# Hybrid pool/mLSTM DiT block on one core: when VectorE makes the modulation sums of the second layer, how their weights are fetched, and how the recurrence's rows lie in DRAM

## The reference, cut to what matters

```python
for i in range(2):                       # x: 1024 tokens x 1024, ctx: 256 tokens x 1024
    sh1, sc1, gt1, sh2, sc2, gt2 = split(silu(c) @ mod_w[i] + mod_b[i])      # 6 x 1024, and again for c_ctx
    hx = rms_norm(x) * (1 + sc1) + sh1   # hc likewise from ctx
    yx = pool_mixer(hx) if i == 0 else mlstm_mixer(hx, hc)
    x = x + gt1 * rms_norm(yx)
    x = x + gt2 * rms_norm(conv_ffn(rms_norm(x) * (1 + sc2) + sh2))
    # layer 0 updates ctx in the same way

def mlstm_mixer(hx, hc):
    qk, v, o, gates = split(h @ w_in)    # 8 heads, 64 wide for q and k, 128 for v
    q, k = split(silu(dwconv(qk)))       # 3x3 taps on the token grid
    # chunks of the sequence: state C, n, m carried from chunk to chunk, forward and backward
    d_w = exp(b[t] - b[s] + ig[s] - m_t);  s = (q @ k.T) * d_w
    h = (s @ v + a_t * (q @ C_prev)) / max(|den|, exp(-m_t))
    return (sigmoid(o) * (h_fwd + h_bwd)) @ w_out
```

## Time and profile before

| | us |
|---|---|
| median of 3 runs | 2312.73 (2310.48 to 2315.27) |
| the profiled execution | 2315.27 |
| its span, first to last instruction | 2313.5 |
| PE busy / DVE busy / ACT busy / POOL busy | 2215.1 / 1514.5 / 1009.1 / 1024.0 |
| mean granted TensorE clock | 0.985 of full speed |

### The profile page before, as it was taken

One profiled execution on the slowest core, in us unless ns is written; L12 is line 12 of the kernel. 1 busy time (PEld: TensorE's weight loads), 2 busy tenths in 40 slices (PEclk: granted clock), 3 DMA queues, 4 the chain that ended last, 5 costly groups with the idle time before them and its releaser, 6 DMA issues.

```text
span 2313.5 us, 35556 instructions
## 1 busy us (share of the span) xinstructions
PE 2215.1 (96%) x13230; PEld 1843.3 (80%) x13230; DVE 1514.5 (65%) x1994; ACT 1009.1 (44%) x1633; POOL 1024.0 (44%) x612
## 2 busy tenths in 40 slices
PE   7989999999999999999899998889999999999997
PEld 5657788888888889998699997767778888888885
DVE  5487566667797735454573536743577777888886
ACT  4653344444444465544332323333464444444443
POOL 0036777777600056652211105630397777771002
PEclk9999999999999999999999999989999999999998
DMA  8764432222381476542242168722112222228352
GB/s 340 249 223 169 159 127 100 82 82 82 132 302 41 163 270 229 168 157 85 97 139 73 61 199 212 208 82 74 64 43 94 82 82 82 109 100 288 131 173 101
DMA packets 144147, 326.85 MB, mean 141 GB/s; under 512 B 11408, under 2 KB 65296, under 8 KB 131728
## 3 DMA queue, kind: packets, MB, share of 16 engines
q1 hardware_dynamic: 126448, 299.87, 38.1%
q10 hardware_dynamic: 17568, 25.17, 3.0%
HBM read 269.82 MB, written 55.18 MB: 140 GB/s over the span
## 4 chain that ended last, share of the span: by engine, by line
PE 86%; DVE 4%; ACT 3%; DMA 3%; POOL 2%; issue 2%; SPq 0%; ACTq 0%; DVEq 0%; POOLq 0%
PE ps L1446 11%; PE ps L1448 11%; PE ps L1447 11%; PE ps L1076 6%; PE ps L1575 6%; PE ps L1078 6%; PE ps L1077 6%; PE ps L1577 5%; PE ps L1576 5%; PE ps L1619 2%; PE ps L1621 2%; PE ps L1620 2%; PE ps L1774 1%; PE ps L1214 1%; PE ps L1350 1%
## 5 line engine op out<-in xcount | busy, mean ns | idle before, releaser
L3117 DVE SCALAR_TENSOR_TENSOR acc<-ps,fcv,acc 128x945 f32<-128x945 f32 (+2 forms) x320 | 391.2, 1222 | 82.2 <-ACT acc L2296 49.6
L3857 POOL TENSOR_TENSOR w_lo<-raw,w_hi 128x2048 fp32r<-128x2048 f32 x36 | 170.2, 4728 | 387.1 <-ACT w_hi L2077 272.7
L3916 POOL TENSOR_TENSOR p_s_lo<-p_s_val,p_s_hi 128x512 fp32r<-128x512 f32 x160 | 242.7, 1526 | 116.0 <-ACT p_s_hi L2240 115.7
L1575 PE MATMUL ps<-da_hi,dw_hi 128*128 128x512 f32 x560 | 218.8, 391 | 0.0
L1576 PE MATMUL ps<-da_hi,dw_lo 128*128 128x512 f32 x560 | 218.1, 389 | 0.0
L1577 PE MATMUL ps<-da_lo,dw_hi 128*128 128x512 f32 x560 | 217.9, 389 | 0.0
L1619 PE MATMUL ps<-w_hi,hx_hi 128*128 128x256 f32 x512 | 146.1, 285 | 4.3 <-ACT stage L2649 4.2
L1621 PE MATMUL ps<-w_hi,hx_lo 128*128 128x256 f32 x512 | 145.6, 284 | 0.0
L1620 PE MATMUL ps<-w_lo,hx_hi 128*128 128x256 f32 x512 | 145.5, 284 | 0.0
L1575 PEld LDWEIGHTS ps<-da_hi,dw_hi 128*128 128x128 f32 x560 | 105.1, 188 | 23.2 <-issue 1.6
L1577 PEld LDWEIGHTS ps<-da_lo,dw_hi 128*128 128x128 f32 x560 | 105.1, 188 | 21.9
(11 more groups left out here) (515 smaller groups left out, 6513.8 us busy)
## 6 DMA issues: line engine op xcount, KB each, us to landing
f_raw<-in_ffn_w SPq DMA_DIRECT2D x25, 1024.0 KB, 5.0
modw<-in_modw SPq DMA_DIRECT2D x48, 512.0 KB, 8.0
raw<-in_ffn_w SPq DMA_DIRECT2D x23, 1024.0 KB, 5.0
a_scr<-fprod SPq DMA_DIRECT2D x40, 512.0 KB, 2.6
land_w<-in_ffn_w SPq DMA_DIRECT2D x40, 512.0 KB, 4.1
f_raw_b<-in_ffn_w SPq DMA_DIRECT2D x18, 1024.0 KB, 5.0
land_b<-a_scr SPq DMA_DIRECT2D x30, 512.0 KB, 5.0
raw<-in_mlstm_w SPq DMA_DIRECT2D x14, 1024.0 KB, 5.1
```

The lines of the kernel that those rows point to most:

```text
L1575: pe.matmul(out, dw_hi[r][:, ws], da_hi[r][:], start=begins, stop=False, skip_group_check=True)
L3117: dve.scalar_tensor_tensor(out, src, cv[:, t:t + 1], out, ALU.mult, ALU.add).then_inc(sem("tap_done"), 1)
L3916: pool.tensor_tensor(p_lo[p][:], src, p_hi[p][:].bitcast(F32), ALU.subtract).then_inc(S.sem("lo_in"), 1)
```

## The change

It has four parts.

- DVE makes the modulation halves in other places: 0 to 3 ahead of all taps, 4 to 7 behind m = 1, 8 to 11 behind m = 3, 12 and 13 behind m = 5, 14 to 19 behind the taps and ahead of the gates, 20 to 23 behind the gates. SP's bursts are placed so that one or two halves always lie loaded ahead.
- The recurrence's rows go to DRAM only for x units and only for the heads' rows, in two new arrays, so that what a unit fetches is one run: 4096 bytes for `dmat`, 2048 for `qa`. There are 7 writes in place of 5.
- All four first `rows_in` are issued together, and the wait for the last `stage` stores moves from ahead of the first one to behind the values of units 4 and 5.
- The transfers of the output weights, `mo_raw` (1 MB) and two of 512 KB into `raw`, move from ahead of unit 6 and ahead of the first values to u = 14, 15 and 16.

```diff
-HALVES_BEHIND = {1: (0, 4), 3: (4, 10), 5: (10, 14)}
-HALVES_LOADED = {2: (0, 2), 6: (2, 6), 7: (6, 12), 9: (12, 16), 13: (16, HALVES)}
+HALVES_BEHIND = {-1: (0, 4), 1: (4, 8), 3: (8, 12), 5: (12, 14)}
+HALVES_LOADED = {3: (0, 6), 5: (6, 10), 7: (10, 14), 9: (14, 16), 11: (16, 20), 12: (20, 22), 13: (22, HALVES)}
...
-            for n, name in enumerate(("gcum", "greset")):
-                sp.dma_start(row_scr[n][:, 0:TC], gk[name][0:64, :]).then_inc(sem("rows_out"), 16)
-                sp.dma_start(row_scr[n][:, TC:NT], gx[name][0:64, :]).then_inc(sem("rows_out"), 16)
+            for dr in range(2):
+                rows = slice(32 * dr, 32 * dr + HEADS)
+                sp.dma_start(decay_scr[dr, 2:NCH].rearrange("n h t -> h n t"), gx["gcum"][rows, :].rearrange("h (n t) -> h n t", t=CH))\
+                    .then_inc(sem("rows_out"), 16)
+                for par in range(2):
+                    rows = slice(32 * dr + par, 32 * dr + HEADS, 2)
+                    sp.dma_start(query_scr[dr, 2:NCH, par].rearrange("n h t -> h n t"), gx["greset"][rows, :].rearrange("h (n t) -> h n t", t=CH))\
+                        .then_inc(sem("rows_out"), 16)
...
-            for K in (K_MOUT, K_MOUT + 1):
-                tile_out(K, a["mlstm_w"][K - K_MIN], K % 2)
...
-            for i in range(2):
-                sp.wait_ge(sem(f"stage_out{i}"), run[i])
...
-                src = row_scr[0, 32 * dr:32 * dr + 8, n * CH:n * CH + CH]
-                sp.dma_start(dmat[:, i % 4], src.unsqueeze(0).broadcast_to([P, HEADS, CH])).then_inc(sem(f"row_in{i % 4}"), 16)
+                src = decay_scr[dr, n].rearrange("h t -> (h t)")
+                sp.dma_start(dmat[:, i % 4].rearrange("p h t -> p (h t)"), src.unsqueeze(0).broadcast_to([P, HEADS * CH])).then_inc(sem(f"row_in{i % 4}"), 16)
...
-            rows_in(x_units[0])
-            rows_in(x_units[1])
+            for i in range(4):
+                rows_in(x_units[i])
             sp.wait_ge(sem("unit_done"), 4)
             values_in(4)
             values_in(5)
-            rows_in(x_units[2])
-            rows_in(x_units[3])
+            for i in range(2):
+                sp.wait_ge(sem(f"stage_out{i}"), run[i])
             for u in range(4, len(units)):
-                if u == 6:
-                    sp.wait_ge(sem("unit_done"), 4)
+                if u == 14:
                     sp.wait_ge(sem("modcol1_ready"), M + 2)
                     sp.dma_start(mo_raw[:], a["mlstm_w"][len(MSEQ) + 2][:, 0:2048]).then_inc(sem("mo_in"), 16)
+                if u in (15, 16):
+                    tile_out(K_MOUT + u - 15, a["mlstm_w"][len(MSEQ) + u - 15], (K_MOUT + u - 15) % 2)
...
+            for n in range(*HALVES_BEHIND[-1]):
+                chunk_half(n)
             for m in range(8):
...
+            dve.wait_ge(sem("q_silu"), 8)
+            dve.wait_ge(sem("kc_silu"), 4)
+            for n in range(14, 20):
+                chunk_half(n)
...
-            dve.wait_ge(sem("kc_silu"), 4)
-            for n in range(HALVES_BEHIND[5][1], HALVES):
+            for n in range(20, HALVES):
                 chunk_half(n)
```

More of the change, by code:

```diff
@@ L272, in build @@
         stage = at("stage", WORK + 28672, [P, 2, 256])
-        NT = NCH * CH
+        ROWS_OUT = 16 * 7
         GA = W_HI
@@ L375, in build @@
         o_scr = scratch("o_scr", (8, P, 1024))
-        row_scr = scratch("row_scr", (2, 64, NT))
+        decay_scr = scratch("decay_scr", (2, NCH, HEADS, CH))
+        query_scr = scratch("query_scr", (2, NCH, 2, HEADS // 2, CH))
         al_scr = scratch("al_scr", (64, NCH))
@@ L593, in build @@
              "step_done": 8, "evicted": 8, "res_added": 8, "half_pair0": 192, "half_pair1": 192, "half_pair2": 192, "half_pair3": 192,
[1 row of a table removed]
+             "half_pair4": 64, "landed0": 16, "landed1": 16, "landed2": 64, "b21_in2": ROWS_OUT, "a_out0": 144, "a_out1": 144,
              "first_pair0": 160, "first_pair1": 160, "first_pair2": 160, "first_pair3": 160, "first_pair4": 160})
@@ L937, in _ @@
             sp.wait_ge(sem("rows_ready"), 3)
-            for n, name in enumerate(("gcum", "greset")):
-                sp.dma_start(row_scr[n][:, 0:TC], gk[name][0:64, :]).then_inc(sem("rows_out"), 16)
-                sp.dma_start(row_scr[n][:, TC:NT], gx[name][0:64, :]).then_inc(sem("rows_out"), 16)
+            for dr in range(2):
[6 more added lines that the diff above has]
+                        .then_inc(sem("rows_out"), 16)
             sp.dma_start(al_scr, gend[0:64, 3, :]).then_inc(sem("rows_out"), 16)
-            sp.wait_ge(sem("rows_out"), 80)
+            sp.wait_ge(sem("rows_out"), ROWS_OUT)
             sp.wait_ge(sem("vo_done"), evac_of[len(MSEQ) - 2][-1] + 1)
@@ L973, in rows_in @@
                     sp.wait_ge(sem("num_done"), i - 3)
-                src = row_scr[0, 32 * dr:32 * dr + 8, n * CH:n * CH + CH]
-                sp.dma_start(dmat[:, i % 4], src.unsqueeze(0).broadcast_to([P, HEADS, CH])).then_inc(sem(f"row_in{i % 4}"), 16)
+                src = decay_scr[dr, n].rearrange("h t -> (h t)")
+                sp.dma_start(dmat[:, i % 4].rearrange("p h t -> p (h t)"), src.unsqueeze(0).broadcast_to([P, HEADS * CH])).then_inc(sem(f"row_in{i % 4}"), 16)
                 for par in range(2):
-                    src = row_scr[1, 32 * dr + par:32 * dr + 8:2, n * CH:n * CH + CH]
-                    sp.dma_start(qa[64 * par:64 * par + 64, i % 4],
-                                 src.unsqueeze(0).broadcast_to([64, 4, CH])).then_inc(sem(f"row_in{i % 4}"), 16)
+                    src = query_scr[dr, n, par].rearrange("h t -> (h t)")
+                    sp.dma_start(qa[64 * par:64 * par + 64, i % 4].rearrange("p h t -> p (h t)"),
+                                 src.unsqueeze(0).broadcast_to([64, 4 * CH])).then_inc(sem(f"row_in{i % 4}"), 16)
             def gates_in(u):
@@ L3675, in _ @@
             dve.wait_ge(sem("cols_ready"), 4)
-            dve.wait_ge(sem("rows_out"), 80)
+            dve.wait_ge(sem("rows_out"), ROWS_OUT)
             dve.wait_ge(sem("vo_done"), len(evacs))
```

## The result

| | before | after |
|---|---|---|
| median | 2311.61 us (2310.18 to 2315.27, 4 runs) | 2296.96 us (2295.55 to 2298.81, 4 runs) |
| the profiled execution | 2315.27 us | 2295.55 us |
| its span | 2313.5 us | 2293.7 us |
| mean granted TensorE clock | 0.985 | 0.990 |

The change makes the kernel faster: the ratio is 0.9935, with a 95% interval of 0.9918 to 0.9952. The forecast was 2295.5 us, with a range of 2289 to 2304. In the change PE's lines stand 3 higher: L1097 is now L1100, L1774 is L1777, L1808 is L1811; in the experiments they shift by a few lines either way.

A forecast was written before the change was run, and what follows sets the result against it. PE was taken as the bound, busy 2215.1 of 2313.5 us. Gains of 12.1 + 4.9 + 1.5 = 18.5 us gave 2296.8 from the profiled execution or 2294.2 from the median; 2295.5 was taken between them, range 2289 to 2304.

The forecast's parts named there:

- Term one: Second context norm in the projections: PE no longer waits for DVE's reciprocal, and its clock stays up; 12.1 us gained.
- Cover of the moved sums: Projections: halves 0 to 3 and 14 to 19 fit into DVE's idle time at their new places; 0 us.
- Early traffic: Near 1042 to 1055 us: four more halves (2 MB) move, yet stores get through; 0 us, bounds -7.4 and +2.5.
- Term two: Early recurrence: the third x unit's rows come earlier, so its 11.20 us become 6.32; 4.9 us gained.
- Term three: Recurrence: rows in long runs shorten transfers, ending PE's wait behind the first gates; 1.5 us gained, bounds 0 and 3.
- output weights later: Recurrence from u = 14: 2 MB more in the queue fit, since gated units take longer; 0 us, bound -2.
- The queue's share: Recurrence: the transfer queue's share falls to about three quarters, a unit's transfers from 6.2 to 4.6 us.
- The rival that long runs are served more slowly: Recurrence: 4096-byte runs across 128 partitions slower than short ones; at 8.5 us a unit, time 2333 us; chance 0.03 (slower).
- A sign of being wrong: Recurrence: the prediction would be wrong if POOL still waits for rows in every unit; no size given.
- recurrence gives little: Rival: queue stays as slow with long runs, or late output weights delay gates; gain 12 to 14, about 2301 us; chance 0.15.
- early traffic: Rival: early loads cost the full 7.4 us in the first `o` tile's evacuations; gain 11.1, 2304 us; chance 0.11.

The follow-up runs named there:

- e3: Kernel before with only the loads of halves 2 and 3 issued one weight tile earlier (behind t = 5, not 6): 2300.32 us, ratio 0.9952.
- e1: Kernel before with only the modulation sums and their loads in the new places: 2301.61 us, ratio 0.9961.
- e4: Changed kernel with the output weights fetched in units u = 7, 9 and 11, not 14, 15 and 16: 2296.39 us, ratio 0.9937.
- e7: Changed kernel with only two units' rows ahead of the values of units 4 and 5, the next two behind them: 2299.11 us, ratio 0.9948.
- e10: Changed kernel repeated unedited, in more rounds: 2298.27 us, ratio 0.9938.
- e12: Changed kernel with the two raw transfers moved from u = 15 and 16, so all output weights at u = 14: 2301.78 us, ratio 0.9959.
- e2: Changed kernel with the modulation sums and their loads at the old places: 2307.22 us, ratio 0.9981.
- e8: Changed kernel with sums at old places, old loads except halves 2 and 3 one tile earlier, output weights at u = 7, 9, 11: 2295.95 us, ratio 0.9938.
- e9: Kernel of e11 with the first two gate transfers issued at u = 11 and 12, not 13 and 14: 2295.32 us, ratio 0.9927.
- e11: Kernel of e8 repeated unedited, in more rounds: 2294.60 us, ratio 0.9925.
- e5: Changed kernel with the output weights back at their old places: 2296.96 us, ratio 0.9945.

## Why the prediction was right, and where it was not

- **Term one** (12.1 us, bounds 9.3 to 12.5) was right in mechanism and in size. B to D fell by 58.93 - 49.46 + 244.24 - 241.12 = 12.6 us. From the last product ahead of the spread to the next one it is 11.42 - 1.04 = 10.4 us less, as forecast; the ten products behind took 2.38 us and not 4.12, so the clock gave 1.7 us there, as forecast too. The 0.5 us left lie elsewhere ahead of D and have no cause that I know. e3 shows that the late load alone was the cause.
- **Cover of the moved sums** (0): right. Halves 0 to 3 were done at 1055.8 (forecast 1055), halves 4 to 7 at 1101.4 (forecast 1100.7), halves 14 to 19 at 1275.0, 3.8 us ahead of the gates. The first two loads landed 12.5 and 13.0 us after their issue, though, later than the 10.7 that I took as the worst; the slack took it up. By e3 this move bought nothing, and the forecast didn't see that; it took the table of sums and that of loads as one.
- **Early traffic** (0, bounds -7.4 and +2.5) is a term that I mis-sized. The profiled pair shows 0.3 us, since the kernel before had a moment of low clock there and the changed one none (0.97 against 1.00 on the mean). Over all kernels A to B is 52.0 us on average where four more halves move early (changed, e1, e4 to e7, e10, e12) and 50.3 where they don't (before, e2, e3, e8, e9, e11): a cost of 1.7 us. PE's waits alone say the same, 3.9 against 2.2 us on average. I had argued that the new loads go one at a time, so that stores get through. The four behind the first two do go so, and the stores still landed later, in 2.5 to 4.6 us and not 1.8 to 1.9, which held ACT and with it PE.
- **Term two** (4.9 us, bounds 3.4 to 5.5): right. The unit's interval fell by 11.20 - 6.33 = 4.9 us, 3.4 of it the wait and the rest the clock (0.86 over that interval before), and e7 gives back 3.5. e1 shows how near the edge the old order was: there the same rows at the same place cost only 0.9 us more than an even unit. Why they landed that much better in e1 I can't say.
- **Term three** (1.5 us) was right by itself, and **output weights later** (0, bound -2) is the step that I had wrong, though its bound held. With the weights at their old places, u14 to u16 takes 18.22 us with old rows (e1) and 16.61 with new ones (e5): 1.6 us for the rows, as the first gates reach POOL 1.9 us earlier. With new rows and late weights it is 18.32, 18.66, 18.00 and 16.82 us (changed, e10, e2, e7), 17.95 on average: 1.3 us lost again, and 3.4 with twice the weights (e12). I had argued that gated units are long enough for 2.8 us of `mo_raw`. They are long enough for values and rows; the second gates are issued behind it and landed after 9.5 us. From 1425 to 1450 the queue's share is 90.5% in the changed kernel and 80.2% in e5, which has no weights there. So this part of the change gives back most of what the long runs win, by the traces; the device times of the changed kernel, e4 and e5 don't tell them apart. In e7, with the same order of issue, the second gates landed after 7.9 us, and that is why it escaped; why they were faster there stays open.
- **The queue's share** was forecast to fall to about three quarters, from 6.2 us of transfers for a unit to 4.6. In the stretch without gates or weights it is 66.9 against 77.2%, 13% less. For a unit that is 0.772 x 6.32 = 4.9 us with the old rows and 4.2 with the new. My price of 2.4 ns a packet came from a stretch with gates, whose packets are larger: 623 bytes on average there, 500 here. Per MB both stretches agree, 0.983 x 25 / 6.35 = 3.9 us and 0.772 x 25 / 5.00 = 3.9; the long runs cost 0.669 x 25 / 5.24 = 3.2. The rival that long runs are served more slowly is out. The Trainium skill, page "DMA: Bandwidth & Descriptors", section "Specifications", gives line rate from 512 bytes on. By that the two forms would have cost the same; the measurement differs, by a fifth.
- **A sign of being wrong** that I had named did show: POOL still waits for rows, 1.9 to 3.7 us in each of the sixth to eleventh x unit. It was a poor sign. PE waits for nothing there, before as after, since POOL is ahead of it by then and sits idle until the next buffer of rows has been freed and filled.
- **The sum.** With the measured terms it is 12.6 + 4.9 + 1.6 - 1.7 - 1.3 = 16.1 us, against 14.7 to 14.9 on the medians; the rest, 1.2 to 1.4 us, I can't place. The 18.5 of the forecast was too high by the two costs. The 19.8 us between the two profiled spans are high by chance: the changed kernel's profile has no low clock in the first two x units, where its repetition e10 has one that costs 1.6 us, and the profiled execution of before was 3.7 us above its median. That the time itself was missed by only 1.5 us is partly luck. The gain was forecast 3.9 us too high, but was taken from 2295.5 + 18.5 = 2314.0 us, between the median and the profiled execution, 2.4 us above what the kernel before took.
- **The rivals.** 14.7 us lies just under my 15 to 22 and just over the 12 to 14 of *recurrence gives little*. The recurrence gave its gain, D to E fell by 7.2 us against a forecast of 6.4; but that rival's late weights did push the gates back, as *early traffic* did cost, at a quarter of its full price.

## What to carry to other kernels

When an engine comes late because it sat in a wait for a load, move the load in the issuing queue's list before anything is moved on the engine: one edit of a table gave 11 of the 14.7 us here, and moving the work as well cost about 1.7, by the stages. A bulk load with no due time belongs where the queue has slack and nothing urgent is issued right behind it; in the first turns of a loop, look for the first use of each new stream (here the gates) and keep bulk out of the two turns ahead of it. Cost a transfer's form by the queue's share in a stretch where only that stream moves, and per MB rather than per packet. To tell what ends last in a pipelined unit, line up all kernels: a difference that stays constant, as the 15.0 us here, names the transfer.

## What was unexpected of the hardware

The granted clock falls for a moment around the first x unit in some executions and not in others of the same program. The changed kernel, first x unit, the first profile (its row stands above with 2.05 us) and its repetition e10:

```profile
1385.38 3.65 PE L1777 MATMUL ps<-vch,dmat 128*128 128x129 f32 x16 [0.41 <-DMA vch<-v_scr]
```

In e10 the granted clock from 1380 to 1390 us is 0.83 on the mean, between full speed and the lower level:

```profile
1380.00:1390.00 10.00, 7.42 (x68) 6.51 (x66) 4.08 (x7) 9.49 (x33) 6.16 (x4) 0.83 0.39 107
```

Ahead of it PE does the same in both, with waits of 2.2 us for `dmat` and 0.2 to 0.4 us for the values. The unit then takes 6.32 to 6.33 us (changed, e5, e8), 6.84 to 6.96 (before, e4, e11) or 7.25 to 7.96 (the others), so 1.6 us come and go with no edit. In e5 the moment lies ahead of the unit, in before, e4 and e11 partly so: from D to the second x unit it is 25.0 us in the changed kernel and e8, and 26.2 to 27.9 in all others. A similar one sits between u = 17 and 19 in the profiles of before and of the changed kernel, an interval of 9.95 us where it is 8.3. What decides it stays open.

SP's issue of a transfer takes longer behind bulk: that of the row transfer took 0.58 us at the start of the changed kernel's recurrence, 1.00 us in the turn with 1 MB of weights ahead, and 3.28 us with 2 MB (e12).
